# Tokens turned by products with diagonal scales, eight products in two blocks, tables a group later, pooling in single steps

## The reference

```python
def hybrid_layer(h, norm_w, w_in, ...):
    xn = rmsnorm(h, norm_w)                 # x * rsqrt(mean(x^2) + eps) * norm_w
    proj = xn @ w_in                        # 2048 -> 14368 columns
    u_pool, z_pool, q, k, v, z_dn, b, a, gate_pool, gate_dn = split(proj)
    y_pool = causal_multiscale_pool(u_pool, pool_mix, pool_scale) * silu(z_pool)
    y_dn = gated_deltanet_branch(q, k, v, z_dn, b, a, ...)   # 16 heads, chunked scan
    merged = sigmoid(gate_pool) * (y_pool @ w_pool_out) + sigmoid(gate_dn) * (y_dn @ w_dn_out)
    return h + merged @ w_o                 # then a final rmsnorm, meta rows dropped

# pooling: 4 groups of 256 channels, trailing mean over 2, 4, 8, 16 rows, minus the row,
#          times a 256x256 matrix per group
# gates:   beta = sigmoid(b), g = -exp(A_log) * softplus(a + dt_bias), summed per chunk
```

## Time and profile before

| what | us |
|---|---|
| median of three runs | 1941.22 (1935.66 to 1942.7) |
| the profiled execution | 1936.51 |
| its span in the trace | 1934.8 |
| TensorE busy | 1848.5 (96%), 15265 matmuls |
| VectorE / ScalarE / GpSimd busy | 1313.6 / 1003.7 / 125.6 |
| TensorE's clock as granted, over the span | 0.99 of full |

### The profile page before, as it was taken

The page is one execution under the profiler, slowest core; times in us unless marked ns, Lnnn a source line. Parts: engine busy times, 40 slices in busy tenths (PEclk is TensorE's granted clock), DMA queues, the critical chain, the costliest instruction groups (busy, mean ns, idle before and its releaser), DMA issues.

```text
span 1934.8 us, 38055 instructions
## 1 busy us (share of the span) xinstructions
PE 1848.5 (96%) x15265; PEld 1732.9 (90%) x15265; DVE 1313.6 (68%) x2420; ACT 1003.7 (52%) x2316; POOL 125.6 (6%) x158
## 2 busy tenths in 40 slices
PE   5889999999999999999999999999999999999998
PEld 4889899989999999989999998999999788888886
DVE  7868758768787786868878687777777544335332
ACT  5444445757566665756667576645456322224232
POOL 2000010101001010100101011000000000000000
PEclk8999999999999999999999999999999999999999
DMA  4323464536555463644536365365644534347202
GB/s 148 99 66 111 110 175 125 145 89 191 137 147 135 131 166 101 189 134 144 143 116 172 108 187 137 92 186 170 173 118 140 188 113 140 117 135 289 101 22 87
DMA packets 311000, 264.90 MB, mean 137 GB/s; under 512 B 12202, under 2 KB 266627, under 8 KB 310179
## 3 DMA queue, kind: packets, MB, share of 16 engines
q1 hardware_dynamic: 284018, 197.35, 35.5%
q0 software_dynamic: 12992, 39.57, 7.5%
q10 hardware_dynamic: 13824, 25.70, 3.7%
HBM read 221.03 MB, written 42.60 MB: 136 GB/s over the span
## 4 chain that ended last, share of the span: by engine, by line
PE 63%; DVE 17%; ACT 7%; issue 6%; DMA 6%; POOL 1%; SPq 0%; ACTq 0%; DVEq 0%; POOLq 0%
PE pj L887 32%; PE pj L818 17%; PE pg L818 8%; DVE wl L1746 4%; ACT wh L1212 3%; PE pt L818 2%; DVE stg L2095 2%; DMA st<-gram_scratch 2%; DVE raw L1779 1%; PE pj L844 1%; DVE st L2150 1%; DVE st L2147 1%; DMA raw<-in_w_in 1%; DMA dec<-in_consts 1%; DVE raw L1762 1%
## 5 line engine op out<-in xcount | busy, mean ns | idle before, releaser
L887 PE MATMUL pj<-xh,wh 128*128 128x256 f32 (+2 forms) x2688 | 788.1, 293 | 43.3 <-DVE wl L1746 15.7
L887 PE MATMUL pj<-xl,wh 128*128 128x256 f32 (+2 forms) x2688 | 762.1, 284 | 0.0
L887 PE MATMUL pj<-xh,wl 128*128 128x256 f32 (+2 forms) x2688 | 761.7, 283 | 0.0
L1746 DVE TENSOR_TENSOR wl<-raw,wh 128x512 fp32r<-128x512 f32 x752 | 506.3, 688 | 299.3 <-ACT wh L1212 292.9
L1212 ACT ACTIVATE wh<-raw 128x512 fp32r<-128x512 f32 x752 | 458.6, 626 | 425.4 <-PE pj L887 195.8
L887 PEld LDWEIGHTS pj<-xh,wh 128*128 128x128 f32 x2688 | 511.2, 190 | 55.0 <-ACT snap L1212 17.6
L887 PEld LDWEIGHTS pj<-xl,wh 128*128 128x128 f32 x2688 | 512.1, 191 | 1.0 <-issue 1.0
L887 PEld LDWEIGHTS pj<-xh,wl 128*128 128x128 f32 x2688 | 510.8, 190 | 0.0
L1212 ACT ACTIVATE bwh<-rawb 128x256 fp32r<-128x256 f32 x192 | 64.9, 405 | 174.3 <-PE pj L818 168.8
L844 PE MATMUL pj<-xh,wh 128*128 128x260 f32 (+1 forms) x512 | 147.3, 288 | 3.4 <-ACT xin L1212 2.8
L818 PE MATMUL pj<-yh,bwh 128*128 128x512 f32 x384 | 150.1, 391 | 0.3 <-DVE yl L2299 0.3
(11 more groups left out here) (301 smaller groups left out, 2432.0 us busy)
## 6 DMA issues: line engine op xcount, KB each, us to landing
raw<-in_w_in SPq DMA_DIRECT2D x224, 512.0 KB, 4.7
head_scratch<-stg ACTq DMA_DIRECT2D x64, 264.0 KB, 3.8
rawb<-in_w_dn_out SPq DMA_DIRECT2D x16, 1024.0 KB, 6.1
rawb<-in_w_o SPq DMA_DIRECT2D x12, 1024.0 KB, 5.5
kq<-head_scratch SPq DMA_DIRECT2D x8, 1056.0 KB, 9.8
gates_scratch<-stg ACTq DMA_DIRECT2D x32, 256.0 KB, 2.0
rawb<-in_w_pool_out SPq DMA_DIRECT2D x8, 1024.0 KB, 5.5
yraw<-branch_scratch SPq DMA_DIRECT2D x6, 1024.0 KB, 7.9
```

The costliest lines, as they stand in the source:

```text
L887: mm = pe.matmul(bank[:, c0:TH], w[:, slot, k, :], xx[what][:, kt, c0:TH], start=opens and one and kt == 0, stop=closes and last and kt == ...
L1746: tt(wl[:, slot, :, :], raw[:, buffer_of(of, par, what), HK * half:HK * (half + 1), :], wh[:, slot, :, :].bitcast(F32), ALU.subtract).then ...
```

## The change

**Turning.** The tile is no longer scaled. VectorE scales a 128x128 identity by the rows' factors (dg), and TensorE multiplies the tile's pieces by it, as ordinary fp32 products, 80 in all, in place of 80 transposes. **Blocks 0 and 1** use the plan of eight products; block 0 makes P1 itself and has 18 chunks (16 before), block 1 has 16 (14 before). The combinations 7, 6 and 4 of the tokens are made during blocks 0 and 1, for block 2; GpSimd makes the low part of one quarter instead of two. **Tables** are made in group 2 instead of group 1, and ScalarE's steps for them are taken apart. **Pooling** is done a single step after each split from step 11 on; the mix product stands two chunks later. **The last gate block** splits one row of y in each of steps 2 to 7, and ten in steps 8 to 11; the output weights a step later. Buffers of the pooling branch lie in another order. Everything else is renamed or folded together.

```diff
-ORDER_FIRST = (1, 2, 7, 6, 4, 5, NEXT, 3)
...
+EIGHT_FIRST = ("eight products, its own P1 first",)
+EIGHT_SECOND = ("eight products, B22 first",)
+EIGHT = ("eight products",)
+REST = ((4, 1, "b"), (4, 5, "c"), (5, 1, "b"), (5, 5, "c"), (6, 3, "c"), (6, 2, "b"), (7, 3, "c"), (7, 2, "b"),
+        (8, NEXT, "other"), (9, NEXT, "other"))
+CHUNKS8 = {
+    EIGHT_FIRST: ((0, 1, "own"), (1, 1, "own"), (2, 2, "own"), (3, 2, "own"), (2, 3, "other"), (3, 3, "other"),
+                  (0, 5, "other"), (1, 5, "other")) + REST,
+    EIGHT_SECOND: ((0, 3, "other"), (1, 3, "other"), (0, 2, "own"), (1, 2, "own"), (2, 5, "other"), (3, 5, "other")) + REST,
+    EIGHT: ((0, 2, "own"), (1, 2, "own"), (0, 3, "other"), (1, 3, "other"), (2, 5, "other"), (3, 5, "other")) + REST}
...
+SPLIT8 = {EIGHT_FIRST: {0: (4,), 7: (5,), 8: (6,), 9: (7,), 10: (8,), 11: (9,)},
+          EIGHT_SECOND: {0: (3, 4), 3: (5,), 4: (6,), 5: (7,), 6: (8,), 8: (9,)},
+          EIGHT: {0: (3, 4), 3: (5,), 4: (6,), 5: (7,), 6: (8,), 8: (9,)}}
+NEXT8 = {EIGHT_FIRST: {12: 0, 14: 1, 16: 2}, EIGHT_SECOND: {10: 0, 12: 1, 14: 2}, EIGHT: {10: 0, 12: 1, 14: 2}}
+TABLES_AT = 2
...
+    if b < 2:
+        return (EIGHT_FIRST, EIGHT_SECOND)[b]
...
+        Y_PARTS = {2: (0,), 3: (1,), 4: (2,), 5: (3,), 6: (4,), 7: (5,), 8: (6, 7), 9: (8,), 10: (9, 10), 11: (11, 12, 13, 14, 15)}
...
-            for slot, quarter in ((RA, 11), (RB, 12), (RE, 21), (RF, 22)):
+            for slot, quarter in ((RA, 11), (RE, 12), (RB, 21), (RF, 22)):
...
-                    if chunk == 0:
+                    if chunk == next(n for n in places["own"] if n > 1 or not is_first(b)):
                         pe.wait_ge(snap_done, snapped(b, "s1"))
...
+                    if is_first(b) and chunk < 8:
+                        if factor == 1:
+                            pe.wait_ge(x_lo_pool, half + 1)
+                        else:
+                            pe.wait_ge(x_lo, {2: 1, 3: 3, 5: 5}[factor] + half)
...
-                mm = pe.transpose(xbanks[0][:, kt * META:(kt + 1) * META], xt[0][0:META, kt * P:(kt + 1) * P], cst[0:META, CI:CI + META])
+                mm = product(xbanks[0][:, kt * META:(kt + 1) * META], xt[0][0:META, kt * P:(kt + 1) * P], dg[0:META, 0, 0:META], True, True)
...
-                        mm = pe.transpose(xbanks[n % 4][:, k * P:(k + 1) * P], xt[i][:, kt * P:(kt + 1) * P], ident)
+                        mm = product(xbanks[n % 4][:, k * P:(k + 1) * P], xt[i][:, kt * P:(kt + 1) * P], dg[:, i % 2, :], True, True)
...
-                        if (z, h) == (1, 16):
+                        if (z, h) == (1, 20):
...
+                    if b == 0 and t == 2 or b > 0 and t == 0 and eight(b - 1):
+                        act.wait_ge(pe_chunk, base_of(b) + t)
+                        copy(snap[:, par, c0:TH], bank_a[par][:, c0:TH]).then_inc(snap_done, 1)
...
-            split_hi(0, 0, 0)
-            split_hi(0, 0, 1)
+            for at in range(2):
+                split_hi(0, 0, at)
+            for half in range(2):
+                act.wait_ge(x_f, 16 + half)
+                x_hi_part(3, half, f22)
+            for at in range(2, 4):
+                split_hi(0, 0, at)
             for half in range(2):
                 act.wait_ge(x_sum, 1 + half)
-                x_hi_part(7, half, fd)
-            split_hi(0, 0, 2)
-            split_hi(0, 0, 3)
-
...
+            def x_his(b, t):
+
+                if b == 0 and t in (9, 10):
+                    act.wait_ge(x_sum, 3 + t - 9)
+                    x_hi_part(7, t - 9, f12)
+                if b == 1 and t in (1, 2):
+                    act.wait_ge(x_sum, 5 + t - 1)
+                    x_hi_part(6, t - 1, f11)
+                if b == 1 and t in (5, 6):
+                    act.wait_ge(x_sum, 7 + t - 5)
+                    x_hi_part(4, t - 5, f21)
 
...
+                if (z, m) == (0, 11):
+                    act.activation(al[:, 0, :], al[:, 0, :], ACT.Exp).then_inc(tab_act, 1)
+                if (z, m) == (0, 14):
                     act.wait_ge(tab_dve, 2)
                     act.activation(tq[:, 1], tq[:, 0], ACT.Abs).then_inc(tab_act, 1)
-                    act.wait_ge(tab_act, 1)
+                    act.wait_ge(tab_act, 2)
                     act.activation(tq[:, 2], tq[:, 1], ACT.Exp, scale=-1.0).then_inc(tab_act, 1)
-                    act.wait_ge(tab_act, 2)
+                if (z, m) == (0, 15):
+                    act.wait_ge(tab_act, 3)
                     act.activation(tq[:, 3], tq[:, 2], ACT.Ln, bias=1.0).then_inc(tab_act, 1)
-                    act.activation(al[:, 0, :], al[:, 0, :], ACT.Exp).then_inc(tab_act, 1)
-                    act.activation(table[:, :, BETA, :], tb[:, 0], ACT.Sigmoid).then_inc(tab_act, 1)
                 if (z, m) == (1, 8):
                     act.wait_ge(tab_dve, 5)
...
-                            act.wait_ge(pe_chunk, last + after(ORDER_LAST, 6))
-                        y_hi_part(k)
-                if t in (8, 9):
+                for k in Y_PARTS.get(t, ()):
+                    if k == 0:
+                        act.wait_ge(yraw_loaded, 80)
+                        act.wait_ge(pe_chunk, last + after(ORDER_LAST, 7))
+                    if k == UK:
+                        act.wait_ge(pe_chunk, last + after(ORDER_LAST, 6))
+                    y_hi_part(k)
+                if t in (9, 10):
...
-                dve.tensor_scalar(xt[i][0:r, :], xt[i][0:r, :], stat[0:r, 2, i:i + 1], None, ALU.mult).then_inc(x_scaled, 1)
+                dve.tensor_scalar(dg[0:r, i % 2, 0:r], cst[0:r, CI:CI + r], stat[0:r, 2, i:i + 1], None, ALU.mult).then_inc(x_scaled, 1)
                 if i >= 1:
                     x_f_part(i - 1)
+            for half in range(2):
+                dve.wait_ge(x_f, 8 + half)
+                x_lo_part(2, half, f21, 3 + half)
...
             dve.wait_ge(x_f, 17)
-            for half in range(2):
-                x_total(fd, f12, f22, ALU.subtract, half)
             split_lo(0, 0, 0)
             split_lo(0, 0, 1)
-            s3(0, 0)
             for half in range(2):
-                x_lo_part(7, half, fd, 5 + half)
-                dve.wait_ge(x_sum, 1 + half)
-                dve.wait_ge(x_lo, 1 + half)
-                x_total(fd, fd, f11, ALU.subtract, half)
-            split_lo(0, 0, 2)
-            split_lo(0, 0, 3)
-
...
+                x_total(fd, f12, f11, ALU.subtract, half)
+                split_lo(0, 0, 2 + half)
+            for half in range(2):
+                x_lo_part(3, half, f22, 5 + half)
+            for half in range(2):
+                x_lo_part(5, half, fd, 7 + half)
+
+            def x_sums(b, t):
+
+                if b == 0 and t in (5, 6):
+                    dve.wait_ge(x_sum, 1 + t - 5)
+                    x_total(f12, f12, f22, ALU.subtract, t - 5)
+                if b == 0 and t in (12, 13):
+                    x_lo_part(7, t - 12, f12, 9 + t - 12)
+                if b == 0 and t in (15, 16):
+                    dve.wait_ge(x_sum, 3 + t - 15)
+                    dve.wait_ge(x_lo_pool, 1 + t - 15)
+                    x_total(f11, f12, f11, ALU.subtract, t - 15)
+                if b == 1 and t in (2, 3):
+                    dve.wait_ge(x_sum, 5 + t - 2)
+                    dve.wait_ge(x_lo, 1 + t - 2)
+                    x_total(f21, f11, f21, ALU.add, t - 2)
+                if b == 1 and t in (5, 6):
+                    x_lo_part(6, t - 5, f11, 11 + t - 5)
+                if b == 1 and t in (9, 10):
+                    x_lo_part(4, t - 9, f21, 13 + t - 9)
 
             def ba_split():
 
...
+            def pooling(g, c, n):
+
+                levels = g + 1
+                adds = g * (g + 1) + (1 - c) * levels + n
+                source = ub[:, c, :] if n == 0 else pa[:, (n - 1) % 2, :]
+                if n == 0:
+                    dve.wait_ge(add_done, added(2 * g, "second" if c == 1 else "C12" if eight(2 * g) else "C11"))
+                    if c == 0:
+                        dve.wait_ge(last_done, 2 * g + 1)
+                    need(dve, mix_mm, g)
+                    need(dve, pool_step, 2 * g + 1 - c)
                 else:
-                    dve.wait_ge(add_done, added(2 * g, "C11"))
...
-                        dve.wait_ge(pool_add, steps[0])
+                    dve.wait_ge(pool_add, adds)
+                if n < levels:
+                    lag = 1 << n
                     lo = 2 * lag - 1
-                    tt(pa[:, n % 2, lo:T], src[:, lo:T], src[:, lo - lag:T - lag], ALU.add).then_inc(pool_add, 1)
-                    steps[0] += 1
-                    src, lag, n = pa[:, n % 2, :], 2 * lag, n + 1
-                dve.wait_ge(pool_add, steps[0])
-                dve.scalar_tensor_tensor(pooled[:, c, :], src[:, META:T], 1.0 / WINDOWS[g], ub[:, c, META:T],
...
+                        if g == 1 and z == 1 and t == 9:
                             ba_split()
                         if g > 0 and z == 0 and t == 3:
                             pool_out(g - 1)
```

(23 more changed lines are left out.)

473 lines of the change are left out of this document (195 added, 278 removed).

## The result

The changed kernel takes 1919.12 us (median of five executions, 1914.85 to 1922.65); the kernel before, on the same chip, 1938.83 (five, 1933.68 to 1942.7). The ratio is 0.9898, 95% interval 0.9873 to 0.9924: 19.7 us, or 1.0%, less. 1920 was forecast. The sum behind it was right by compensation: the start was too large by 3.0 us, the middle and the last gate block were too small by 1.6 each, and another 1.6 came from a stage that had no term.

A forecast was written before the change was run, and what follows sets the result against it. TensorE, busy 96% of the span, bounds the kernel. Start 7.5, tables 6.7, pooling 4.3, returned waits -1.0 and last gate block 2.5 sum to 20.0 us won: 1921.2, taken as 1920; range 1911 to 1931.

The forecast's parts named there:

- (a): First token tile at the start: TensorE begins at 11.3, narrow products take 3.8 us, tile ends at 15.1.
- (b): Four wide tiles of 16 products: 0.25 us each, 0.44 before full pace at 18; third tile ends at 28.4.
- (c): First chunk: VectorE's remaining work after the third wide tile takes 6.1 us, so it stands at 34.5.
- (d): Third chunk waits for ScalarE's snap until 40.0, a pause of 2.5, with 1.0 for the lower clock after it.
- (e): Then 16 chunks each of blocks 0 and 1 and mix products: block 1 ends at 90.2, not 97.8.
- The tables: TensorE's snap wait at 130 us: one of four table loads left ahead; 6.7 us won, not below 4.5.
- The pooling: TensorE's waits for wl in groups 2 and 3, together 5.1: single steps win 4.3, from 3 to 5.1.
- The last gate block: TensorE's 2.91 wait for a sum and the slow clock behind it go; 2.5 us won, between 4.3 and -0.8.
- my two cases: Last gate block: C11's store takes 2.0 or 5.5 us, so the last-y product begins at 1500.1 or 1503.6.
- The turning did stay at the lower clock: Rival: all 64 turning products at the lower clock, nothing won at the start; 12.5 in all, 1928; chance 0.12.
- Returned waits: Rival: y's load costs all the end's gain, tables and pooling cost 4, not 1; 14.5 in all, 1926; chance 0.14.
- the fourth rival: Rival, slower: turning products' weight loads and matmuls do not overlap; break-even 0.69 each, at 0.9 1951 us; chance 0.03.

The follow-up runs named there:

- second trace: The changed kernel run once more, unaltered: 1916.18 us (six executions), ratio 0.9901 to the kernel before.
- experiment 3: The changed kernel with 14 plain fp32 identity products added while TensorE waits for the parameters: 1916.73 us, ratio 0.9885 to the kernel before.
- experiment 2: The changed kernel with all token tiles scaled on VectorE and transposed again: 1914.76 us, ratio 0.9882 to the kernel before.
- experiment 9: The changed kernel with the narrow tile transposed, snap between xh5's halves, and C11 ahead of the last y splits: 1913.49 us, ratio 0.9872 to the kernel before.
- experiment 11: The changed kernel with all five tiles transposed, snap between xh5's halves, and C11 ahead of the y splits: 1914.07 us, ratio 0.9871 to the kernel before.
- experiment 1: The kernel before with only the turning changed to products: 1940.97 us against 1938.17, ratio 1.0017.

## Why the prediction was right, and where it was not

**(a) First tile: failed.** The start at 10.65 was earlier than 11.3 by luck: counted from TensorE's first instruction it is 1.64, as in the second trace (11.59 less 9.95), and was 2.70, so the scaling saved 1.06 where I had 1.16. But the tile lasted 7.0 us and not 3.8. I took twice the transpose's 0.118 of the earlier trace rows, though that row's engine was not yet at its full pace, which I knew from the wide transposes behind it (0.22 each). A record of the narrow transposes is short at the lower pace, one of the narrow products is not: it comes at the wide one's 0.22, and there are two. At the full clock it comes at 0.11 (experiment 3), again like a wide one. Why, no run shows. Experiments 2 and 9 show the sizes: 1.8 us by transposes, 7.0 by products.

**(b) Four tiles: failed in the clock, right in the price.** I took the full pace at 18, from "6.5 us after the first transpose". But narrow products held TensorE until 17.6, and the pace came at 21.9, behind 4.3 us of wide ones; with the narrow tile by transposes (experiment 9) it came at 17.7. At the full pace a product is 0.223 (16 in 3.57), a bit below the 0.25 of the earlier trace rows, and at the lower 0.44 as taken. The third wide tile was done at 30.6, not 28.4.

The rule of the Trainium skill that I held against the trace ("TensorE: Matmul & The Clock Gate", Part 4: transposes do not count as the engine being busy in the same way, and the full clock does not come with them) is not borne out here either. With transposes alone (experiment 11) the pace doubled at 18.1, when wide ones had run since 14.39, and with products (experiment 9) at 17.7, when wide ones had run since 13.77. The rule in the Terms of that page, that the transpose mode is four times faster for fp32, does not hold for the wide tiles: 0.22 against 0.11 is twice. For the narrow ones, 7.0 against 1.8, it does, at the low clock.

**(c), (d): right.** 6.1 forecast from the third tile to the first chunk, and it was 6.3; 5.5 forecast from there to the third chunk, and it was 5.4, with 2.2 of pause for the snap and 1.6 of slow clock, where I had 1.0. **(e)** From the third chunk to block 2: 50.2 forecast, 51.1 measured. So the whole miss of the start, 3.0, is 2.45 from (a) and (b) and the rest from (e); without the earlier transfer it would be some 0.75 more. One row was misread on the way: the VectorE operation of 2.82 in the earlier trace rows did not end with GpSimd's first low part but 1.1 behind it (see the last section). Behind it all stands what I did not ask: does the turning itself pay? It doesn't (experiments 1, 2). The rest of the start's change pays for it: with the turning undone, block 2 begins 9.9 earlier than in the kernel before (87.93; 0.7 of it is the earlier transfer). I put this down to the plan of eight products, but that plan was not run by itself.

**The tables:** 6.7 forecast, 4.9 alone and 5.9 as undone in the changed kernel. 1.7 and 1.1 of wait remained and not 0.5: alone, 0.99 for ScalarE's snap and 0.71 for VectorE's part (tq); in the changed kernel VectorE's part only. **The pooling:** 4.3 forecast, 5.4 and 5.3. Its effect on the tables' snap, 1.3 us, was counted with the tables; the waits that I set against both, 1.0, are 1.5 in the trace (at 173.10 and 226.48).

**The last gate block:** 2.5 forecast, 4.1 measured. TensorE was 5.4 earlier (5.8 forecast). C11 ended where it did, its store took 2.0, and 7.1 lie between load and product (1475.49 and 1482.60): the favourable of my two cases. Its wait of 1.8 came in two pieces, 0.82 and 0.95, so the single wait of 2 to 5 that I had named as a sign did not. I had put the likeliest value between the two cases. The other is not excluded: in experiment 2 the store took 3.7 and TensorE waited 2.60, and in experiment 3 the product came 9.4 behind the load and TensorE waited 3.15.

**The rivals.** The turning did stay at the lower clock for the 16 narrow and some 10 wide products, not for all. Returned waits cost 1.5 in the middle, where this rival had 4, and 1.4 at the end, where it had all of the gain. A wide product costs two transposes, not four, and 0.22 is far from the 0.69 of the fourth rival's break-even. In the chances there is a slip: the first three and a third of the fourth come to 0.90, not 0.87.

**The 1.6 us in the heads** were in no term: there the kernel before lost two stretches of 1.6 to the clock (278, 394) and the changed one none, and somewhat longer waits and other small differences took half of it back. They are luck of the two profiled executions, not a gain of the change: in the second trace of the changed kernel there are two stretches in that place.

## What to carry to other kernels

Price an operation at the start by the pace that its row has, and ask at which pace the engine was when the row was taken: here the narrow tile cost 1.8 us as transposes and 7.0 as products. Before a time at the start is called won, set it against the moment when the first transfer landed in each trace. An edit that is carried by a larger one has to be tried by itself: the turning lost 3 to 4 us (by the first chunk and the medians) inside a change that won 20. Where TensorE is busy for 96% of the span, a pause of 2 us costs itself and, in some executions, 1.6 us more, so several small pauses are worth taking apart even when each alone disappears in the spread.

## What the runs showed of the hardware that I had not expected

- In a_warm TensorE was busy without a gap from 10.49, with pieces of 16 rows and columns until 16.3, behind a pause of 1.14, and the granted clock went from 1.00 to 0.50 at 11.7 and stayed there until 22.0.
- The granted clock reads 1.00 from the start of a trace, while matmuls start at half the rate (x7 in a window, then x12). Until the first change of it, the count in a window is the better clock.
- Pauses of the same length and place end in a slow stretch in one execution and not in the next: 2.85 at 278 and 2.84 at 262 (second trace) did, 3.06 at 262 (first trace) did not. A pause of 1.79 at 394 in the kernel before did too.
- A VectorE operation that scales 128x128 took 1.04 where its equals took 0.29, when it began beside a low part on GpSimd; it ended just behind that part. It is the same in every trace with products. The operation of 2.82 in the earlier trace rows, from 22.67, is like it: its equals took 1.29, and GpSimd's first low part ended at 24.41. GpSimd's second, which was due then, took 3.39 and not 2.4, beside the rest of it:

```profile
26.40 2.44 POOL L2419 TENSOR_TENSOR xl<-f,xh 128x1056 fp32r<-128x1056 f32 x1 [25.83 <-ACT xh L1205]
```

```profile
24.38 3.39 POOL L2430 TENSOR_TENSOR xl<-f,xh 128x1056 fp32r<-128x1056 f32 x1
```

The first row is of the changed kernel, the second of the kernel before. The Trainium skill, "SBUF — State Buffer", "SBUF: two separate sides", describes an exclusive lock on a port pair that VectorE, in its two-port modes among others, and GpSimd share, where the later one waits for the whole instruction. The traces agree, in both directions: 27.88 + 1.04 is 28.92, and GpSimd's operation ended at 28.84.
